# The triangular solve of a chunked RWKV-7 recurrence on blocks of 32 instead of 64

## The reference, cut to what matters

```python
def wkv7_scan(r, w, k, v, a, b):
    def step(state, inp):
        r_t, w_t, k_t, v_t, a_t, b_t = inp
        sa = jnp.einsum("bhvk,bhk->bhv", state, a_t)
        state = (state * w_t[:, :, None, :]
                 + sa[..., None] * b_t[:, :, None, :]
                 + v_t[..., None] * k_t[:, :, None, :])
        return state, jnp.einsum("bhvk,bhk->bhv", state, r_t)
    ...

def first_block(x, mem, ...):
    h = rms_norm(x, norm_mix[i])
    p = h @ w_in[i]                                  # r, k, v, decays, gates, convolution inputs
    ...
    y = wkv7_scan(rh, wh, kh, vh, -kk, kk * ah)      # inside rwkv7_branch
    ...                                              # cross attention, MLP; then second_block
```

## Time and profile before

| | us |
|---|---|
| device time, median of 3 runs | 1412.94 (1411.88 to 1413.27) |
| device time of the profiled execution | 1413.47 |
| its span, first to last instruction | 1412.2 |
| PE busy | 1393.5 (99%), 8982 matmul records |
| DVE busy | 814.5 (58%) |
| ACT busy | 479.1 (34%) |
| POOL busy | 136.8 (10%) |
| mean granted TensorE clock | 0.997 of full speed |

### The profile page before, as it was taken

The page is one execution under the profiler, slowest core; times in us unless marked ns, Lnnn a source line. Parts: engine busy times, 40 slices in busy tenths (PEclk is TensorE's granted clock), DMA queues, the critical chain, the costliest instruction groups (busy, mean ns, idle before and its releaser), DMA issues.

```text
span 1412.2 us, 20873 instructions
## 1 busy us (share of the span) xinstructions
PE 1393.5 (99%) x8982; PEld 1112.5 (79%) x8982; DVE 814.5 (58%) x1134; ACT 479.1 (34%) x723; POOL 136.8 (10%) x138
## 2 busy tenths in 40 slices
PE   7999999999999999999999999999999999999998
PEld 5687887878778888887778888887887877888886
DVE  7374654746548755354575674556635435767754
ACT  6332324234135333234431221323243232443323
POOL 1020302002002011001210000000040011003000
PEclk9999999999999999999999999999999999999999
DMA  5110201111042333322255543232221333212262
GB/s 190 59 46 32 76 32 60 47 46 61 32 164 90 105 120 119 105 75 75 90 179 194 194 164 101 93 97 93 86 100 65 98 97 104 90 61 75 79 174 90
DMA packets 42205, 136.18 MB, mean 96 GB/s; under 512 B 4650, under 2 KB 8362, under 8 KB 42113
## 3 DMA queue, kind: packets, MB, share of 16 engines
q1 hardware_dynamic: 33984, 114.57, 24.9%
q0 software_dynamic: 4080, 14.68, 2.8%
q10 hardware_dynamic: 4048, 5.59, 1.1%
HBM read 130.37 MB, written 2.10 MB: 94 GB/s over the span
## 4 chain that ended last, share of the span: by engine, by line
PE 95%; DVE 2%; DMA 1%; ACT 1%; issue 1%; ACTq 0%; DVEq 0%
PE bank L417 93%; PE bank L420 2%; DMA w_raw<-panels 1%; DVE opA_lo L1426 1%; DMA xT<-x 1%; DVE w_lo L1418 0%; DVE tmp L1426 0%; ACT scores L928 0%; DVE P L1426 0%; ACT w_hi L928 0%; DVE scores L1418 0%; ACT opA_hi L928 0%; DVE tmp L1418 0%; DVE x_tokens L1426 0%; DVE pad L1418 0%
## 5 line engine op out<-in xcount | busy, mean ns | idle before, releaser
L1418 DVE TENSOR_TENSOR w_lo<-w_raw,w_hi 128x1024 fp32r<-128x1024 f32 (+1 forms) x209 | 257.4, 1232 | 348.0 <-ACT w_hi L928 347.7
L417 PE MATMUL bank<-opA_hi,w_hi 128*128 128x512 f32 x1000 | 410.8, 411 | 10.2 <-DVE opA_lo L1426 8.2
L417 PE MATMUL bank<-opA_hi,w_lo 128*128 128x512 f32 x1000 | 395.7, 396 | 0.0
L417 PE MATMUL bank<-opA_lo,w_hi 128*128 128x512 f32 x1000 | 394.6, 396 | 0.0
L928 ACT ACTIVATE w_hi<-w_raw 128x1024 fp32r<-128x1024 f32 (+1 forms) x209 | 220.1, 1053 | 368.3 <-DMA w_raw<-panels 368.1
L417 PEld LDWEIGHTS bank<-opA_hi,w_hi 128*128 128x128 f32 x1000 | 188.1, 188 | 64.6 <-issue 16.4
L417 PEld LDWEIGHTS bank<-opA_hi,w_lo 128*128 128x128 f32 x1000 | 188.3, 188 | 45.6
L417 PEld LDWEIGHTS bank<-opA_lo,w_hi 128*128 128x128 f32 x1000 | 188.5, 189 | 41.6 <-issue 2.2
L417 PE MATMUL bank<-opB_hi,w_hi 128*128 128x512 f32 x448 | 178.5, 398 | 0.3 <-DVE w_lo L1418 0.3
L417 PE MATMUL bank<-opB_hi,w_lo 128*128 128x512 f32 x448 | 177.2, 395 | 0.0
L417 PE MATMUL bank<-opB_lo,w_hi 128*128 128x512 f32 x448 | 177.2, 395 | 0.0
(11 more groups left out here) (317 smaller groups left out, 1624.5 us busy)
## 6 DMA issues: line engine op xcount, KB each, us to landing
w_raw<-panels SPq DMA_DIRECT2D x208, 512.0 KB, 3.3
ada_w<-ada POOLq DMA_DIRECT2D x24, 512.0 KB, 4.5
xT<-x ACTq DMA_DIRECT2D x1, 2048.0 KB, 14.5
x_tokens<-x_blocks SPq DMA_DIRECT2D x16, 128.0 KB, 4.0
out<-x_tokens SPq DMA_DIRECT2D x8, 256.0 KB, 2.0
memT<-mem ACTq DMA_DIRECT2D x1, 1024.0 KB, 5.7
xT<-x ACTq DMA_DIRECT2D x3, 256.0 KB, 7.5
xT<-x SPq DMA_DIRECT2D x3, 256.0 KB, 7.3
```

Source lines behind the costliest of these rows:

```text
L417: return pe.matmul(o, lhsT, rhs, start=start, stop=stop, skip_group_check=True)
L1418: return ve.tensor_tensor(o, a, b, op)
```

## The change

The 64x64 inverse is made of two diagonal blocks of B = 32 rows each and one block below the diagonal. Levels 2 to 16 stay inside the diagonal blocks, so X, Y and a new tile `XT_blocks` (XTb) hold only 32 columns per chunk: 4 blocks (2 heads by 2 halves) in the four groups of 32 partitions. The 16 matmuls of 64x64 by 64 of each set become 32 matmuls of 32x32 by 32, each block in its own rows and columns of the array (`BLOCKS`). At level 32 the set has 16 matmuls of 32x32 by 32, which make only the block below the diagonal; its mask goes (a plain copy), and DVE copies the result into `XT[lo:lo+32, :, 32:64]`. ACT gets eight small copies for each tile `f`: four make XT_blocks out of the bank that ABT comes from, four put the finished diagonal blocks into `XT` after level 16. POOL clears XT once at the start; its two operations on XT work on half the elements. The first product of a and b is made only for the diagonal blocks (32 matmuls of K = 64, 32x32 out). `y_squared` moves by one buffer.

```diff
-            for dst, left_, right in ((3, AR, BK), (4, BK, AR)):
-                for c in range(NC):
+            for c in range(NC):
+                for e in (0, B):
                     for lo, hi in HH:
-                        ins = mm(bank[dst][lo:hi, c * L:(c + 1) * L], left_[lo:hi, c, 0:L], right[lo:hi, c, 0:L])
-                ins.then_inc(ab_mm, 1)
+                        ins = mm(bank[3][lo + e:lo + e + B, c * B:(c + 1) * B], AR[lo:hi, c, e:e + B],
+                                 BK[lo:hi, c, e:e + B])
+            ins.then_inc(ab_mm, 1)
+            for c in range(NC):
+                for lo, hi in HH:
+                    ins = mm(bank[4][lo:hi, c * L:(c + 1) * L], BK[lo:hi, c, 0:L], AR[lo:hi, c, 0:L])
+            ins.then_inc(ab_mm, 1)
...
-                        for lo, hi in HH:
-                            ins = mm(bank[2 + 2 * g][lo:hi, q * L:(q + 1) * L], ABT[lo:hi, c, :], X[lo:hi, c, :])
+                        if n < len(LEVELS) - 2:
+                            for lo, hi, e in BLOCKS:
+                                ins = mm(bank[2 + 2 * g][lo:hi, q * B:(q + 1) * B], ABT[lo:hi, c, e:e + B], X[lo:hi, c, :])
+                        else:
+                            for lo, hi in HH:
+                                ins = mm(bank[2 + 2 * g][lo + B:hi, q * B:(q + 1) * B], ABT[lo:lo + B, c, B:L],
+                                         X[lo:lo + B, c, :])
...
-                            for lo, hi in HH:
+                            if last:
+                                for lo, hi in HH:
+                                    ins = mm(bank[6 + g][lo:lo + B, q * B:(q + 1) * B], Yt[lo + B:hi, c, :],
+                                             XTb[lo + B:hi, c, :])
+                                continue
+                            for lo, hi, _ in BLOCKS:
                                 if turned:
-                                    ins = mm(bank[6 + g][lo:hi, q * L:(q + 1) * L], Yt[lo:hi, c, :], XT[lo:hi, c, :])
+                                    ins = mm(bank[6 + g][lo:hi, q * B:(q + 1) * B], Yt[lo:hi, c, :], XTb[lo:hi, c, :])
...
-            pe.wait_ge(xt_level, 10 * f + 10)
+            pe.wait_ge(xt_level, 12 * f + 12)
+            pe.wait_ge(xt_copied, 9 * f + 9)
...
-            act(ABT[:, :, :], c8(bank[4][:, :]), ACT.Copy).then_inc(abt_done, 1)
+            act(ABT[:, :, :], c8(bank[4][:, :]), ACT.Copy).then_inc(xt_copied, 1)
+            for lo, hi, e in BLOCKS:
+                act(XTb[lo:hi, :, :], c8(bank[4][:, :])[lo:hi, :, e:e + B], ACT.Copy).then_inc(xt_copied, 1)
...
-            p.steps(5 * F_SOLVE + F_Z)
+            p.steps(4 * F_SOLVE)
+            ac.wait_ge(xt_level, 12 * f + 8)
+            if f == 0:
+                ac.wait_ge(ones, 2)
+            for lo, hi, e in BLOCKS:
+                act(XT[lo:hi, :, e:e + B], XTb[lo:hi, :, :], ACT.Copy).then_inc(xt_copied, 1)
+            p.steps(F_SOLVE + F_Z)
...
         gp.memset(Pb[:, :, 0:1], 1.0).then_inc(ones, 1)
+        gp.wait_ge(lora_mm, 3 * FT)
+        gp.memset(XT[:, :, :], 0.0).then_inc(ones, 1)
...
-            ve.wait_ge(ones, 1)
+            ve.wait_ge(ones, 2)
...
-                    tt(Yt[:, 4 * g:4 * g + 4, :], bank[2 + 2 * g][:, 0:4 * L].rearrange("p (c l) -> p c l", c=4),
-                       wide(f"level{s}", 4), ALU.mult).then_inc(y_done, 1)
+                    ps = bank[2 + 2 * g][:, 0:4 * B].rearrange("p (c l) -> p c l", c=4)
+                    if last:
+                        ve.tensor_copy(Yt[:, 4 * g:4 * g + 4, :], ps).then_inc(y_done, 1)
+                    else:
+                        tt(Yt[:, 4 * g:4 * g + 4, :], ps, wide(f"level{s}", 4), ALU.mult).then_inc(y_done, 1)
...
+                        if last:
+                            for lo, hi in HH:
+                                ve.tensor_copy(XT[lo:lo + B, d, B:L], ps[lo:lo + B]).then_inc(xt_level, 1)
+                        else:
+                            tt(o[:, d, :], o[:, d, :], ps, ALU.add).then_inc(xt_level if turned else x_level, 1)
```

More of the change, by code:

```diff
@@ L45 @@
 LEVELS = [1, 2, 4, 8, 16, 32]
+B = L // 2
 MATS = [("ident", 128), ("mean", 128), ("head_sum", 128), ("cumsum", 128), ("chunk_mask", 128),
-        ("rotate", 128), ("causal", 128), ("eye", 64), ("level1_turned", 64)] + [(f"level{s}", 64) for s in LEVELS]
+        ("rotate", 128), ("causal", 128), ("eye", B), ("level1_turned", B)] + [(f"level{s}", B) for s in LEVELS[:-1]]
 MAT = {}
@@ L58, in constants @@
     i, j = np.arange(128)[:, None], np.arange(128)[None, :]
-    j64 = np.arange(64)[None, :]
+    jb = np.arange(B)[None, :]
     same = (i // 64) == (j // 64)
@@ L68, in constants @@
         "causal": i <= j,
-        "eye": (i % 64) == j64,
+        "eye": (i % B) == jb,
     }
[L71 to L74, removed]
+    for s in LEVELS[:-1]:
+        ii = i % B
+        out[f"level{s}"] = (ii // (2 * s) == jb // (2 * s)) & ((ii // s) % 2 == 1) & ((jb // s) % 2 == 0)
+    out["level1_turned"] = np.tile(out["level1"][:B].T, (4, 1))
     return np.concatenate([out[n].astype(np.float32) for n, _ in MATS], axis=1)
@@ L243, in build @@
     UV = place("UV", [NP, NC, NP], r_sg + 4096)
-    X = place("X", [NP, NC, L], r_p + 12 * TB)
+    X = place("X", [NP, NC, B], r_p + 12 * TB)
+    XTb = place("XT_blocks", [NP, NC, B], r_p + 12 * TB + TB // 2)
     XT = place("XT", [NP, NC, L], r_p + 13 * TB)
-    Yt = place("Y", [NP, NC, L], r_p + 14 * TB)
+    Yt = place("Y", [NP, NC, B], r_p + 14 * TB)
     Z = place("Z", [NP, NC, L], r_p + (GATE0 + 3 * FT - 1) * TB)
@@ L255, in build @@
     HH = [(0, 64), (64, 128)]
+    BLOCKS = [(B * b, B * (b + 1), B * (b % 2)) for b in range(4)]
     memT = place("memT", [NP, KT, N_MEM], r_p + 4 * TB)
@@ L1336, in gpsimd_program @@
             gp.memset(st[0][:, :], 0.0).then_inc(state_zero, 1)
-            gp.wait_ge(abt_done, f + 1)
-            tt(XT[:, :, :], ABT[:, :, :], wide("level1_turned", NC), ALU.mult).then_inc(xt_done, 1)
+            gp.wait_ge(xt_copied, 9 * f + 5)
+            tt(XTb[:, :, :], XTb[:, :, :], wide("level1_turned", NC), ALU.mult).then_inc(xt_done, 1)
             gp.wait_ge(xt_done, 2 * f + 1)
-            tt(XT[:, :, :], XT[:, :, :], wide("eye", NC), ALU.add).then_inc(xt_done, 1)
+            tt(XTb[:, :, :], XTb[:, :, :], wide("eye", NC), ALU.add).then_inc(xt_done, 1)
             p.steps(F_WKV - F_WKV_END)
@@ L1677, in vector_program @@
             ve.wait_ge(ab_mm, 2 * f + 1)
-            tt(X[:, :, :], c8(bank[3][:, :]), wide("level1", NC), ALU.mult).then_inc(x_made, 1)
+            tt(X[:, :, :], c8(bank[3][:, 0:NC * B]), wide("level1", NC), ALU.mult).then_inc(x_made, 1)
             ve.wait_ge(x_made, 2 * f + 1)
@@ L1706, in vector_program @@
                             ve.wait_ge(xt_done, 2 * f + 2)
-                        o, b = (XT, 6 + g) if turned else (X, 3 + 2 * g)
-                        tt(o[:, d, :], o[:, d, :], bank[b][:, 0:4 * L].rearrange("p (c l) -> p c l", c=4),
-                           ALU.add).then_inc(xt_level if turned else x_level, 1)
+                        o, b = (XTb, 6 + g) if turned else (X, 3 + 2 * g)
+                        ps = bank[b][:, 0:4 * B].rearrange("p (c l) -> p c l", c=4)
+                        if last:
[3 more added lines that the diff above has]
+                            tt(o[:, d, :], o[:, d, :], ps, ALU.add).then_inc(xt_level if turned else x_level, 1)
             p.steps(F_Z)
```

10 lines of the change are left out of this document (5 added, 5 removed).

## The result

| | before | after |
|---|---|---|
| device time, median of 4 runs on the same chip | 1412.67 (1411.88 to 1413.27) | 1437.27 (1437.03 to 1438.64) |
| span of the profiled execution | 1412.2 | 1436.0 |
| mean granted TensorE clock | 0.997 | 0.985 |

The ratio is 1.0179 [1.0164, 1.0193]. The kernel is 1.8% slower; I had forecast 1.4% faster, 1393 us, and the time lies above the range that I gave, 1386 to 1422 us.

What follows compares the result with a forecast made beforehand. PE, busy for 99% of the span, was taken as the bound. 1413.5 - 19.2 (thirteen doubled sets) - 3.2 (level 32) + 1.1 (shape changes) + 0.8 (DVE lateness) = 1393.0 us, range 1386 to 1422.

Steps and rivals of the forecast that it cites:

- The bound: Whole kernel: PE's instruction stream sets the end, so each us added or removed there counts almost in full.
- A doubled set: Solve and first product: a set of 64 records takes 0.56 us instead of 0.93, saving 0.37.
- the thirteen doubled sets: First product plus Y and X sets of levels 2 to 16, in four tiles: 19.2 us saved.
- 2.7 us a level: Solve: PE's time for a shortened level, down from 3.84 us.
- PE can't be fed: Rival for the doubled sets: records arrive too slowly; 1463 us at 29 ns each, 1434 at 21; chance 0.22.
- The rule that I weighed: Skill rule against the forecast: matmul starts at least about 25 ns apart, so a doubled set takes 1.6 us.
- The last level: Level 32's y and x sets, 16 smaller matmuls each: 0.40 us saved a set, 3.2 in all.
- Changes of shape: PE's stops where tile shape changes: two new ones a tile at 0.14 us, 1.1 us added.
- DVE: 0.29 us for an operation: Solve: DVE operations on 128 columns take 0.29 us, where 256 columns take 421 ns.
- ACT's copies: Eight new copies a tile at 0.37 us each, 3 us a tile, costing nothing; at worst 1 us a tile.
- What I said would show an unfed PE: Sign in the trace after: a doubled set of 1.3 us or more from start to start.
- The other sign that I named: Granted clock below 0.99, or projections outside the recurrence moving, would mean the sum is of the wrong thing.

Runs made afterwards that it cites:

- e6: The kernel before with 12 one-column matmuls over 32 rows, results unread, added behind each Y set of levels 2 to 16; 1416.32 us, ratio 1.0028.
- e1: The changed kernel with the Y and X sets of levels 2 to 16 made for only two of the four blocks; 1392.86 us, ratio 0.9868.
- e4: The kernel before with only level 32 cut to the one 32x32 block below the diagonal, no matmuls added; 1408.76 us, ratio 0.9981.
- e3: The changed kernel with four panel steps instead of one at each solve level, taken from behind the solve; 1415.66 us, ratio 1.0030.
- e7: The kernel before with four panel steps instead of one at each solve level, as control for e3; 1412.14 us, ratio 0.9999.
- e9: e4 with level 16's set that adds to X also made for the first diagonal block only; 1409.22 us, ratio 0.9973 to before.
- e2: The changed kernel with 64 moving columns instead of 32 in the Y and X sets of levels 2 to 16, same instruction count; 1433.14 us, ratio 1.0153.
- e5: The kernel before with 48 one-column matmuls over 32 rows, results unread, added behind each Y set of levels 2 to 16; 1442.29 us, ratio 1.0216.
- e8: The changed kernel with the first product of a and b back as 64x64 matmuls, masked by DVE; 1442.41 us, ratio 1.0204.

## Why the prediction was wrong

The bound. Right: PE set the end, every us in its stream counted, and DVE, ACT and POOL had slack. But "every us of PE's stream" was taken for time of the array. The stream's other limit shows as "issue" in PE's waits. It stood at 0.9 us before and gave no warning: e6, with a block used up in 4.24 us, shows no more of it than before, and the changed kernel 28.8 us.

A doubled set: 0.56 us. Right for the array on the whole. At full clock and without a stop, a set ahead of another takes 0.54 to 0.66 us (0.55 from 104.85 to 105.40), one ahead of a panel step 0.68 to 0.72 where it took 1.03 before, and the first product 0.69 where it took 0.98, so 0.29 saved instead of 0.37. E1 has 0.52 for half of the records. So four tiles do run at once, and the earlier trace rows was read rightly.

The step that failed is its last sentence but one: "I take 0.56, near the first, since the earlier trace rows shows a third tile joining without the others slowing down." It answers whether the array can take the records, and it let that stand for whether they can be brought. The term that hangs on it, - 19.2 us for the thirteen doubled sets, is what didn't come out. Before, a level has 99 records, 198 instructions, in 3.84 us, 256 in 4.97. With my 2.7 us a level and 195 records it would be 390 instructions, 256 in 1.8 us. The runs show that they come no faster than 256 in about 3.5 to 4 us: with 1.1 us before each packet, 0.96 to 1.45 for it and 1.2 to 1.4 behind it, PE stood still for 27.9 us in the solves. I had the number of instructions in hand ("with its weight load each is two instructions") and used it only for a price per record.

The rival "PE can't be fed" came out, at a chance of 0.22; its 1434 us at 21 ns a record are near the 1437 measured. The nearness is partly luck. It isn't a slower rate of records: they run at 9 ns each (0.55 / 64) until the block is used up, and then stop for up to 2.5 us. And a part of the loss is the clock, which the rival hadn't. What I said against it ("21 ns came out of tiles that had no more to do, not out of a queue that ran dry") was true of these rows and said nothing on the rate over several us.

The rule that I weighed, 25 ns between starts of matmuls (the Trainium skill, TensorE: Matmul & The Clock Gate, part 1), isn't what happened: 64 records in 0.55 us are 9 ns apart.

The sum in terms: I had - 22.4 for sets, + 1.1 for shapes, + 0.8 for DVE, 20.5 less. In the solves, which hold twelve of the thirteen sets, my terms are 4 * (19.97 - 14.87) = 20.4 less; on top of them came 28.0 us of stops and 13.3 us of longer busy time, and 2.9 us elsewhere. - 20.4 + 28.0 + 13.3 + 2.9 = + 23.8, the difference of the spans. The 13.3 us I put down for the most part to the half clock, since the rows at 115.45 and 117.03 show a panel step 0.67 us and a set about 0.3 us longer at 0.50. In the four windows PE is busy for 26.8 us at a granted clock of 0.50; with the panel step's share, 0.67 of 1.58, that is 11.4 us, an estimate. The last record before each of the 18 stops is also listed with its whole 0.2 us, up to 3.6 us in all. No run took the clock away with the stops left as they are, so this share is worked out and not shown.

The last level: saving 0.40 a set, 3.2 in all. Right: e4, where no stops interfere, measures 3.0, and its rows have 0.62 where 1.03 stood.

Changes of shape: + 0.14 each. About right: A_t's turn ahead of the first set of 32x32 takes 1.08 us from start to start (96.98 to 98.06), where it took 0.98 before (97.15 to 98.13), so 0.10.

DVE: 0.29 us for an operation. Right (289 ns). ACT's copies: 0.37 forecast, 0.39 and 0.43 measured (1.56 / 4 and 1.73 / 4), hidden all the same. POOL: nothing, as forecast.

What I said would show an unfed PE (a set at 1.3 us and more) was too narrow a sign: most sets stay far below that (0.54 to 0.72 us at full clock), and about one in three has a stop in it. The other sign that I named, a granted clock below 0.99, did come.

## What to carry to other kernels

Before splitting small matmuls into more of them that run side by side, count the engine's instructions in blocks of 256, weight loads among them (an fp32 matmul is four), and compare the time that the stream takes for a block with what the chip has shown: here 3.28 us a block left a few stops, 4.24 none, and 1.8, my forecast's rate, stopped PE for more than the split had saved. Splits that keep the number of instructions and shrink each of them are safer, as long as a block still lasts about 4 us (e4: no stops, and 3.0 us less for one level); where more instructions are needed, put denser and sparser work in turn, within a block's length (e3 went part of this way; the rest is advice that no run here tried). And when "issue" turns up as a wait in the middle of a product, take the distances between the ends of the stops before looking at the product: if the distances stay when the work in between changes, it isn't the product. Where a trace has the instruction queue's packets, lay their landings beside the ends of the stops.

## What the runs showed of the hardware that I had not expected

- Blocks of instructions. PE runs 256 instructions (128 fp32 records with their weight loads) and then waits; in the first solve, stops end 3.46 to 4.00 us apart with 32 columns (0.55 us a set) and 3.46 to 3.73 with 64 (0.92 us a set). All 80 stops in the solves of the six kernels that have any end 1.2 to 1.6 us after a 16 KB packet of the instruction queue has landed. Between 103.49 and 114.68 there are three blocks: 14.6 ns an instruction over the long run, whereas within a block they go at 4.3 ns (0.55 us / 128).
- The clock falls in kernels that stop. In the first solve the granted clock is 1.00 to 112.00, with three stops before, and 0.50 from 113.00 to 118.60, through the rest of the fourth stop, which begins at 112.30, and for at least 3.9 us after PE has started again at 114.68. At 112.00 to 112.30 it is still 0.98, at 112.30 to 112.60 it is 0.50. The stops come first, so the clock isn't their cause. The mean clock is 0.997 or 0.998 in the profiles without them (before, e4, e6, e7, e9), and with them 0.995 in e1 (1.9 us of stops in the solves) and in e2 (16.4), 0.992 in e3 (15.0), 0.991 in e5 (8.7), 0.985 in the changed kernel (27.9) and 0.978 in e8 (27.5), so not in proportion to them.
- Four 32x32 tiles run at once: 64 records in 0.55 us, against 0.52 for 32 records in two tiles (e1).
- Matmuls of one weight column by one moving column over 32 rows aren't nearly free: 96 records in about 0.9 us (e5), 9 to 10 ns each, as much as those of 32 columns cost in four tiles.
